# Expert weights with four adjacent rows to a partition: runs of 16 KB instead of 4 KB

## The reference, cut to what matters

```python
logits = h @ w_router + b_router                  # h: (256, 1024)
top_logit, top_idx = lax.top_k(logits, TOP_K)     # 4 of 32 experts a token
gates = softmax(top_logit)
# for every expert e, for the tokens xb that chose it:
g = minimum(xb @ w_gate[e] + b_gate[e], 7.0)      # w_gate[e]: (1024, 1024)
u = clip(xb @ w_up[e] + b_up[e], -7.0, 7.0)
act = g * sigmoid(1.702 * g) * (u + 1)
y = act @ w_down[e] + b_down[e]                   # added to the token's row, times its gate
```

## Time and profile before

| | |
|---|---|
| median of the runs | 3219.16 us |
| the profiled execution | 3218.91 us |
| its span | 3217.4 us |
| mean granted TensorE clock | 0.906 |
| TensorE matmul busy | 2742.5 us (85%) |
| VectorE busy | 865.7 us (27%) |
| the loops of the experts | from about 438 to 1470 us of the span |

### The profile page before, as it was taken

How to read it: one execution, slowest core, us unless ns; L and a number is a source line. 1 busy time by engine, 2 the same in 40 slices (tenths; PEclk the granted TensorE clock), 3 DMA queues, 4 the chain that set the end, 5 groups by cost and what they waited for, 6 DMA issues and landing times. The chain is left out here.

```text
span 3217.4 us, 29638 instructions
## 1 busy us (share of the span) xinstructions
PE 2742.5 (85%) x11507; PEld 1694.2 (53%) x11507; DVE 865.7 (27%) x1931; ACT 312.4 (10%) x617; POOL 23.5 (1%) x39
## 2 busy tenths in 40 slices
PE   0497769999999999997999839995998999766998
PEld 0353344343443433435877527774776776743776
DVE  7423232121121111211371344223553001133001
ACT  0110111000010010101122000001000000021000
POOL 0000000000000000000000000000000000000000
PEclk9897769999999999998989959997998999877999
DMA  7410059999999999994425178625893443311443
GB/s 276 185 60 0 3 218 409 410 410 410 410 410 410 409 410 410 409 394 176 144 92 209 36 271 293 246 94 177 298 345 138 165 156 109 145 52 37 148 155 111
DMA packets 268041, 743.24 MB, mean 231 GB/s; under 512 B 9126, under 2 KB 102708, under 8 KB 266964
## 3 DMA queue, kind: packets, MB, share of 16 engines
q1 hardware_dynamic: 252148, 679.60, 55.5%
q0 software_dynamic: 15840, 62.92, 5.1%
HBM read 741.44 MB, written 1.05 MB: 231 GB/s over the span
## 5 line engine op out<-in xcount | busy, mean ns | idle before, releaser
L1916 PE MATMUL bank<-hT,ffn_wgu 128*128 128x256 f32 x2816 | 625.2, 384 | 29.7 <-DMA ffn_wgu<-in_ffn_w_gu 26.8
L1916 PEld LDWEIGHTS bank<-hT,ffn_wgu 128*128 128x128 f32 x2816 | 540.7, 193 | 125.1 <-issue 42.8
L1221 PE MATMUL bank<-tiled_raw,tiled_xs 128*64 128x512 f32 x2112 | 470.3, 603 | 1.5 <-ACT tiled_xs L1303 1.5
L1221 PEld LDWEIGHTS bank<-tiled_raw,tiled_xs 128*64 128x64 f32 x2112 | 149.4, 142 | 339.8 <-issue 339.0
L1930 PE MATMUL bank<-ffn_wd,ffn_actT 128*128 128x512 f32 x704 | 308.6, 592 | 0.0
L1221 PE MATMUL bank<-tiled_raw,tiled_act_s 128*64 128x512 f32 x1056 | 240.7, 598 | 34.9 <-DMA tiled_raw<-in_w_down 34.9
L1529 PE MATMUL bank<-hT,second_ring 128*128 128x256 f32 x1024 | 223.1, 381 | 4.0 <-DMA second_ring<-in_w_in 4.0
L1979 DVE TENSOR_TENSOR ffn_actT<-ffn_silu,bank 128x256 f32<-128x256 f32 x88 | 36.9, 421 | 698.9 <-ACT ffn_silu L1959 698.9
L1930 PEld LDWEIGHTS bank<-ffn_wd,ffn_actT 128*128 128x128 f32 x704 | 133.8, 190 | 151.3 <-issue 149.2
L1529 PEld LDWEIGHTS bank<-hT,second_ring 128*128 128x128 f32 x1024 | 195.7, 191 | 31.2 <-issue 4.4
L1221 PEld LDWEIGHTS bank<-tiled_raw,tiled_act_s 128*64 128x64 f32 x1056 | 70.1, 136 | 182.1 <-issue 119.6
(11 more groups left out here) (424 smaller groups left out, 2016.5 us busy)
## 6 DMA issues: line engine op xcount, KB each, us to landing
tiled_raw<-in_w_gate SPq DMA_DIRECT2D x66, 2048.0 KB, 20.7
tiled_raw<-in_w_up SPq DMA_DIRECT2D x66, 2048.0 KB, 23.9
tiled_raw<-in_w_down SPq DMA_DIRECT2D x66, 2048.0 KB, 23.5
ffn_wgu<-in_ffn_w_gu SPq DMA_DIRECT2D x88, 1024.0 KB, 9.8
ffn_side_w<-in_mod_w POOLq DMA_DIRECT2D x30, 2048.0 KB, 12.1
ffn_wd<-in_ffn_w_down SPq DMA_DIRECT2D x44, 1024.0 KB, 5.2
second_ring<-in_w_in SPq DMA_DIRECT2D x16, 2048.0 KB
mod_w<-in_w_mod SPq DMA_DIRECT2D x6, 4096.0 KB, 15.4
```

The source lines that it names most:

```text
L1221: last = nc.tensor.matmul(bank[b][h * HALF:(h + 1) * HALF, :], stationary(kt), raw[p][:, k, h * C:(h + 1) * C], start=kt == 0, stop=kt == ...
L1916: last = nc.tensor.matmul(bank[b][:, m * SEQ:(m + 1) * SEQ], wgu[:, s, m, k, f * P:(f + 1) * P], core.hT[:, k, :], start=k == 0, stop=k == ...
```

## The change

A constant `ROWS = 4` is added, and the DRAM side of the weight loads is read as `(p k) n`: partition p now receives the four adjacent rows 4p, 4p+1, 4p+2 and 4p+3 of the half matrix, which in DRAM are one run of 16 KB. The buffer in SBUF has the same shape, and 16 KB of it in a partition are one run too. The number of loads, their size and order stay.

Row 4p+k of the half matrix now lies in partition p of block k. For the contraction to match, the other operand must have its features in the same order: block k of `xs` and of `act_s` must hold features 4p+k. The function `adjacent(k)` gives these columns as a slice of step 4 (16 bytes). `gather` and `turn` take their stationary operand through it. The bias rows are put in the same order by numpy before the launch. `down` needs its hidden features in the same order, and has them from `turn`.

```diff
+ROWS = 4
+        def adjacent(k):
+            first = k // ROWS * ROWS * P + k % ROWS
+            return slice(first, first + (P - 1) * ROWS + 1, ROWS)
...
-                    nc.sync.dma_start(raw[p][:], ins[names[m]][which, 4 * q * P:(4 * q + 4) * P, :]
-                                      .rearrange("o (k p) n -> p (o k) n", p=P)).then_inc(landed[p], 16)
+                    nc.sync.dma_start(raw[p][:], ins[names[m]][which, ROWS * q * P:ROWS * (q + 1) * P, :]
+                                      .rearrange("o (p k) n -> p (o k) n", p=P)).then_inc(landed[p], 16)
...
-                    last = nc.tensor.transpose(bank[b][:, j * P:(j + 1) * P], rows[:, j * P:(j + 1) * P], core.ident[:])
+                    last = nc.tensor.transpose(bank[b][:, j * P:(j + 1) * P], rows[:, adjacent(j)], core.ident[:])
...
-                            last = nc.tensor.matmul(bank[X][:, k * SLOTS:(k + 1) * SLOTS], part[:, t, k * P:(k + 1) * P],
+                            last = nc.tensor.matmul(bank[X][:, k * SLOTS:(k + 1) * SLOTS], part[:, t, adjacent(k)],
...
+            if name in ("b_gate", "b_up"):
+                a = np.ascontiguousarray(a.reshape(-1, P, ROWS).transpose(0, 2, 1))
             ins[name] = give(name, a.reshape(shape))
```

## The result

The changed kernel takes 3337.82 us (median of 4 runs, 3333.57 to 3339.80) against 3219.97 us of the kernel before. The ratio is 1.0364, 95% interval [1.0346, 1.0382]: 3.6% slower. Forecast were 3182 us. The likeliest rival on the other side, slow weight loads at a step of 16 bytes, had been priced at 3324 us.

The account below looks back on a forecast made before the run. The prediction took DMA at 410 GB/s as the bound, with TensorE next: 3218.9 us minus 37 (waits of 34.9, clock shift 2) gives 3182 us, chance 0.62. Its own range was 3172 to 3192, the overall range 3155 to 3222.

Parts of the forecast that it names:

- The likeliest rival on the other side: Gather and both turns per item: weight loads at 16-byte steps take double time, 4.5 us a turn, 3324 us; chance 0.17.
- What bounds the kernel now: Steady loop: DMA binds at 410 GB/s, turns of 30.72 us; TensorE waits 1.15 us a turn for down weights.
- The loads: Weight loads of a turn: 16 KB runs bring them to 29.1 us, bounds 28.9 and 30.7.
- TensorE becomes the bound at 29.5 us: Steady turn: TensorE alone needs 29.4 to 29.6 us, more than the loads' 29.1, so it caps the gain.
- the third rival: Loop turns: TensorE loses less to half clock, needs 28 to 29 us, loads bind at 28.9; 3163 us, chance 0.10.
- The strided weight loads: Gather's 32 and turn's 8 weight loads a turn at 16-byte steps: taken as 0, bounds 0 and 4.5 us.
- the VectorE rows: L1090, L1082, L1091 and L1350: reads 128 bytes apart show no price for the step at 1.1 ns an element.
- the point from which the step decides: Gather and turn: 1.15 us of slack over 40 loads, 29 ns a load; beyond it the kernel is slower than before.
- The second hint: L1221's moving side takes columns at 0.43 ns, twice as fast as weights, so weight loads ask memory half as often.
- My bound: Upper limit for the strided weight loads: twice the time, 40 x 112 = 4.5 us a turn.
- The transposes: The two `turn` of each item: 8 strided weight loads a turn, taken as 0, at most twice the time.
- Biases, SyncE's issues, ScalarE: Biases reordered before launch, 0 on chip; SyncE's issues get shorter, cost nothing; ScalarE got no separate price.

Follow-up runs that it names:

- Experiment 9: Low part of the token matrix left out of the gather: on the kernel before 3218.20 us, on experiment 3 3164.31 us, one run each.
- experiment 5: The kernel before with only the transposes in `turn` reading at a step of 16 bytes: 3224.12 us, ratio 1.0001.
- experiment 8: The changed kernel with two adjacent rows to a partition in place of four, runs of 8 KB and steps of 8 bytes: 3192.63 us, ratio 0.9910.
- experiment 2: The changed kernel with gather and turn reading adjacent columns again, runs of 16 KB kept, operand features not matching: 3182.37 us, ratio 0.9873.
- experiment 4: Experiment 3 with ScalarE reading PSUM at the step when copying gate and up rows, so the transposes read adjacent columns: 3176.65 us, ratio 0.9863.
- experiment 3: The changed kernel with the token matrix written before the loop in the gather's order, so the gather reads adjacent columns; turn keeps its step: 3181.26 us, ratio 0.9868.
- experiment 6: The kernel before with gather block k reading its stationary columns at a step of k+1 elements, turn's four transposes at 1 to 4: 3285.69 us, one run.

## Why the prediction was wrong, point by point

- **What bounds the kernel now** (the loads, 410 GB/s, 1.15 us of slack a turn): right. Experiment 9 shows it with 4 KB runs, experiment 5 shows the slack at work.
- **The loads**: packets of 16 KB, right, 21228 of them. The rate was taken from one 12 us row and a line through two points, 29.1 us a turn. Measured is 29.4, at 428 GB/s. The line itself was sound, its input was not: 8 KB gave 422 over 840 us (experiment 8), and from 410 and 422 the same working gives a fixed part of 9 ns a packet, 612 ns for 16 KB and 428 GB/s, as measured. The 427 of a window of 12 us was not the rate of a long stretch.
- **TensorE becomes the bound at 29.5 us**: wrong too. With the steps out of the way the loads keep the bound: TensorE waits 17.4 us of 840 in experiment 2 and 16.5 in experiment 4, 0.6 us a turn, so that its own turn is about 28.7 us, 0.8 less than I took. In experiment 4 a turn takes 27.8 us where the clock stays up, and the next has a wait for the loads again. The timeline of experiment 4:

```profile
1015.40 0.44 PE L1266 MATMUL bank<-ident,tiled_gated 128*128 128x128 f32 x2
...
1027.39 1.99 PE L1275 MATMUL bank<-tiled_ys,tiled_spread 64*128 64x512 f32 x8
...
1043.19 0.44 PE L1266 MATMUL bank<-ident,tiled_gated 128*128 128x128 f32 x2
...
1049.10 3.65 PE L1229 MATMUL bank<-tiled_raw,tiled_act_s 128*64 128x512 f32 x16 [1.24 <-DMA tiled_raw<-in_w_down]
...
1056.90 3.49 PE L1275 MATMUL bank<-tiled_ys,tiled_spread 64*128 64x512 f32 x8
```

  The scatter of one turn takes 1.99 us, that of the next 3.49. This is the mechanism of the third rival (TensorE gets faster too and the loads bind again), which I had set at 0.10, and it is what happened in experiments 2 to 4. The rival's 3163 us had the loads at 28.9 us a turn; with their 29.4 it comes out near 3178, 1.3 x 31 = 41 us below the kernel before. That my sum gave 3182 for experiment 2 is luck: two errors of opposite sign, loads slower and TensorE faster than taken.
- **The strided weight loads**, "I take 0, as the VectorE rows say": this is the step that failed. Measured are 233 - 112 = 121 ns for each of the gather's 32 loads, 3.9 us a turn, four times the 29 ns that I had named as the point from which the step decides. Both rows that I leaned on were of the wrong kind. The first, shows an engine that asks for an element each 1.1 ns, in single instructions, and it is not the read that I took it for. L1090 and L1091 go over 32 experts with the 2 token tiles innermost, so the 128 bytes lie between the two tiles, and the next expert is 4 bytes on: the 64 elements lie on about 16 lines and not on 64. The prediction's "a line of its own for each element" is not so. (The slope of 1.1 ns also puts the 49 elements of L1082 beside a copy.) The second hint, that a weight load asks half as often as the moving side and so has room, is refuted: the moving side at the same step takes double as well, and the weight load has no room either. My bound (twice the time) was close to the measured value, 224 against 233 ns; I held its chance at 0.17 although the rule on memory lines that I had quoted said it would be so. With no row of TensorE to set against it, it should have had an even chance.
- **The transposes** were in the same bound at twice their time. They take 0.15 us a turn more, not 0.9 (experiment 5).
- **The rival's price** was 4.5 us a turn and 3324 us. The gather's 3.9 and the transposes' 0.15 are less than that; what made up for it is 0.34 + 0.40 us at half clock behind a gather twice as long, which the rival did not have. The mechanism was the rival's.
- **Biases, SyncE's issues, ScalarE**: no cost, right.

## What to carry to other kernels

A change that makes one side of a transfer contiguous often moves the step to another reader; find out what that reader pays before the time is summed, and if its own engine has no row for it, give the bound that decides the sign its full weight. For TensorE in fp32, keep at least two needed elements on each 16 bytes, on both sides of a matmul (only the weight loads of the transposes came off nearly free here). A reordering is cheapest where the data is written once, or on an engine that reads at a step for free: here four ScalarE copies and four VectorE subtractions before the loop, at 597 and 691 ns each as before, turned 3338 us into 3181.

## What the runs showed of the hardware

- A weight load of 128 fp32 columns takes 192 to 197 ns at steps of 4 and 8 bytes, 257 to 261 at 12, 314 to 336 at 16 to 32, in fp32 as in fp32r. A matmul's moving side of 512 columns takes 609 and 612 ns at 4 and 8 bytes, 1068 and 1097 at 16 and 32.
- The weight loads of the transposes behave otherwise. In the kernel of experiment 6 they take 141 ns at step 1, but already 194 at step 2, then 201 and 208, while the transposes stay 0.11 to 0.12 us apart. Why is open.
- ScalarE and VectorE paid nothing for reading PSUM at a step of 16 bytes: 597 ns a copy with and without it (experiments 3 and 4), 691 ns a subtraction (experiment 3). What VectorE pays in SBUF with one element on a line no run shows.
- DMA from HBM in loads of 2 MB: 410 GB/s with runs of 4 KB, 422 with 8 KB, 428 with 16 KB, each at a DMA share of 1.00 to 1.03 over 840 us. From 4 to 16 KB is worth 4.4%.
- In the kernel before the clock falls to 1.2 GHz right behind the gather of 32 short matmuls, each with its weight load, though TensorE is busy there without a break. With that gather of 3.7 us the steady turns all lost the same (a scatter of 3.44 us); with turns of other lengths some lose nothing (1.99 against 3.49 us of scatter); with the gather at 7.6 us the fall begins within it and lasts into the products.
- Half clock and the step don't add up in a weight load. Where the clock falls inside a gather of adjacent columns (experiment 2, granted 0.55 from 1026.8 to 1028.4 us), its last matmuls are 0.21 us apart instead of 0.11. The gather at a step of 16 bytes is at 0.23 at either clock.
